# A two-block transformer in one program: four product tiles per norm, and the residual read from PSUM

## The chip, the cores and the metric

The kernel runs on one core of one Trainium2 chip. The metric is the device time in microseconds of the whole program. The runs of the kernel before took 2886.63 us in the median of three (2885.67 to 2890.1).

The core's engines run side by side and are joined by semaphores: TensorE (PE) multiplies, VectorE (DVE) and ScalarE (ACT) work elementwise and can read PSUM, GpSimd (POOL) works elementwise on SBUF, SyncE (SP) issues the DMAs. Each engine carries out its own program strictly in the order in which it is written.

## The reference, cut to what matters

Two blocks follow each other on 256 tokens of width 1024. The first has two layers, and carries 256 context tokens beside the 256 latent ones (512 columns in all, transposed: features on partitions, tokens on columns):

```python
for layer in range(2):
    x, ctx = ffn_sublayer(x, ...), ffn_sublayer(ctx, ...)        # f0, f2
    o = even_mixer(...) if layer == 0 else odd_mixer(...)        # DeltaNet and conformer / attention
    x = deepnorm_residual(x, mods[5] * o_lat, g, b)              # context too in layer 0
    x = ffn_sublayer(x, ...)                                     # f1, f3; context too in layer 0

def deepnorm_residual(x, y, g, b):
    return layer_norm(DEEPNORM_ALPHA * x + y, g, b)
def ffn_sublayer(x, shift, scale, gate, w_gu, w_down, g, b):
    y = swiglu(modulate(x, shift, scale), w_gu, w_down)          # 1024 -> 2 x 2816 -> 1024
    return deepnorm_residual(x, 0.5 * gate * y, g, b)
```

`modulate` is x * (1 + scale) + shift, `shift`, `scale` and `gate` come from a product of a condition vector with `ada_w`, 9 x 1024 values per layer. So behind each of the six sublayers stands: product, times gate, plus ALPHA times x (ALPHA is the square root of 2), layer norm over the features, modulation, next product. The second block has two layers with attention of three kinds, RMS norms and no ALPHA. All products are wanted in float32 quality.

## The kernel before, in words

**Products.** A weight tile is 128x128. Both the weights and the activations are split into a rounded high part and a rest, and `linear` issues three matmuls for each tile (lines 1570 to 1572: high by high, high by rest, rest by high). One output tile of 128 features takes 8 weight tiles (k = 0 to 7, or 22 in a down projection) and gathers in one of eight PSUM banks, handed out in turn by `Rot`.

**Weights.** All tiles come in the order of use from one stream in chunks of 1024 columns. A chunk has two halves of 512 columns, that is four tiles each. `take` hands out tiles; on entering a new half h it first yields a `load` (every second half) and then, through `splits_ahead`, the `split` of half h + 3, for there are four split buffers (NSPL) and the one it needs was used by half h - 1. A split is one ScalarE copy (line 1884) and one VectorE subtraction (line 2120; in the second block every second one is on GpSimd, line 2579).

**One order for all engines.** The generator `order` yields the steps of the whole program once, and each engine walks through the same list and carries out its part of every step. So the place of a step in `order` is its place in the program of every engine. What must not hold up the products is put into the list `later` and yielded by `run_later` behind the next `linear` or `pair`.

**Feed-forward `ffn` (f0 to f3).** First `pair` runs gate and up of tile m = 0 side by side: for each k a tile of the one, then of the other. Then for m = 1 to 21 `linear` gate, `linear` up, and `glu` (ScalarE Silu, line 1922, VectorE product, line 2202), and `dual`, the rounding of the result into its two parts (ScalarE line 1888, GpSimd line 2584). Then eight down projections of 22 k each. Beside the products a second generator, `ada_vec`, works out later modulation vectors on VectorE (line 2145); `linear` calls one piece of it at every fourth k (`pos["auto"]`), and ahead of m = 18 `drain` runs what is left. A sum on TensorE (line 1620) ends each group of 512 values.

**Residual.** Behind each down or output projection `residual`: ScalarE copies the bank times the gate column into a temporary (line 1916, two pieces of 256 columns where there are 512), VectorE forms ALPHA * x + t (line 2197), then `Sums.add` squares on ScalarE (line 1903) and adds up x and its square (GpSimd line 2588; for the last k VectorE, line 2156).

**Norm.** `Sums.finish`: column sums of both accumulators on TensorE into one bank with one signal (line 1630), `moments` on VectorE (mean line 2163, variance), square root on ScalarE (line 1911), reciprocal (line 2173), and two spreads, which bring a column back to all 128 partitions by TensorE (line 1636). Then for each k: VectorE subtracts the mean (line 2214), multiplies by the root's inverse (line 2220) and modulates 256 columns (line 2225), ScalarE the other 256 (line 1928), and `dual` rounds. `ln_update` turns X itself into the norm's output (line 1941) and goes into `later`; the eight of them stand behind the following `pair`.

**Even mixer.** After its norm `pair` runs the gate columns (`ab`) and `qkv_mm` 0; then for twelve tiles m: `short_conv` (ScalarE copies the bank, line 1960, VectorE five taps, lines 2304 and 2307, ScalarE Silu, line 1963), a part of the gate arithmetic on 64 partitions (`gate_chain`; a reciprocal at line 2252), the square and column sum of the tile before (`l2norm`), and one `linear` of `glu_v`, `glu_g` or `z`.

**Odd mixer.** `flush` runs the updates of X at once; then `load_memory` (SP, line 1537) loads the second block's memory into the half of X that the context held, and waits for the last update. `headnorm` runs `linear` for K0, then K1 (512 columns each), their squares and sums; V; later Q0 to Q7 with 256 columns.

## Time and profile before

| | |
|---|---|
| Median of three runs | 2886.63 us |
| Profiled execution | 2885.58 us, its span 2883.8 us |
| PE busy | 2680.6 us (93%) |
| DVE busy | 1731.7 us (60%) |
| ACT busy | 1260.8 us (44%) |
| POOL busy | 671.8 us (23%) |
| Products L1570 to L1572 | 3880 of each, 1344.2, 1313.4 and 1312.9 us |
| Splits, DVE L2120 | 838, 678.0 us |
| Splits, ACT L1884 | 1024 (of the ring), 623.6 us |
| Mean granted clock of TensorE | 0.949 |

PE's matmuls are pipelined, so the rows of successive ones overlap: in a full stretch one of 512 columns starts each 0.23 us though its row says 0.39. A row of the timeline is its start, its time, the engine, the line, the operation, output and inputs, and in brackets the idle time of the engine just before it with what released it. Rows of the same kind that follow each other are merged (xN).

### The profile page before, as it was taken

How to read it: one execution, taken by the hardware profiler on the slowest of the kernel's cores; microseconds unless marked ns; L12 is line 12 of the kernel's file. 1: busy time of each engine (PE TensorE's matmuls, PEld its weight loads, DVE VectorE, ACT ScalarE, POOL GpSimd, SP SyncE). 2: the span in 40 equal slices, each digit the busy share in tenths (PEclk: the TensorE clock that was granted, in tenths of full speed). 3: DMA queues.
4: the chain of work that ended last, by engine and by line, in shares of the span. 5: the costliest groups of instructions: out<-in, count | busy, mean ns of one | idle time of the engine just before them, and what ended most of it. 6: DMA issues, size and time to landing. Idle time of an engine off the chain costs nothing.

```text
span 2883.8 us, 43361 instructions
## 1 busy us (share of the span) xinstructions
PE 2680.6 (93%) x16824; PEld 2313.4 (80%) x16824; DVE 1731.7 (60%) x2978; ACT 1260.8 (44%) x2390; POOL 671.8 (23%) x608
## 2 busy tenths in 40 slices
PE   8999997988788999999999988989979999899998
PEld 5887886867776888887888867789978988898888
DVE  5775666778766765556554555565544656346666
ACT  3332326531255333334333345655545575454673
POOL 1111111012134111112111121021134424555224
PEclk9999998998788999998999988999979999899999
DMA  6553441210002543433443422245524434334334
GB/s 252 184 175 115 153 154 44 81 59 2 2 16 74 179 168 127 144 128 117 161 153 124 168 81 74 81 139 184 183 88 135 145 109 133 131 132 139 117 104 138
DMA packets 115868, 352.85 MB, mean 122 GB/s; under 512 B 12752, under 2 KB 14928, under 8 KB 115280
## 3 DMA queue, kind: packets, MB, share of 16 engines
q1 hardware_dynamic: 115664, 350.08, 36.1%
q8 instruction: 134, 2.20, 0.3%
q14 instruction: 70, 0.57, 0.1%
HBM read 348.98 MB, written 1.05 MB: 121 GB/s over the span
## 4 chain that ended last, share of the span: by engine, by line
PE 72%; DVE 12%; ACT 7%; issue 5%; POOL 3%; DMA 1%; SPq 0%; DVEq 0%; ACTq 0%; POOLq 0%
PE ps L1570 20%; PE ps L1572 19%; PE ps L1571 19%; ACT spl L1884 2%; PE ps L1620 2%; DVE spl L2120 1%; DVE big L2330 1%; PE ps L1636 1%; DVE work L2307 1%; PE ps L1838 1%; PE ps L1630 1%; DVE work L2225 1%; ACT big L2061 1%; POOL bigr L2584 1%; PE ps L1581 1%
## 5 line engine op out<-in xcount | busy, mean ns | idle before, releaser
L1570 PE MATMUL ps<-bigr,spl 128*128 128x256 f32 (+1 forms) x3880 | 1344.2, 346 | 69.9 <-issue 21.2
L1571 PE MATMUL ps<-bigr,spl 128*128 128x256 f32 (+1 forms) x3880 | 1313.4, 339 | 0.0
L1572 PE MATMUL ps<-bigr,spl 128*128 128x256 f32 (+1 forms) x3880 | 1312.9, 338 | 0.0
L2120 DVE TENSOR_TENSOR spl<-ring,spl 128x512 fp32r<-128x512 f32 x838 | 678.0, 819 | 652.8 <-ACT spl L1884 650.2
L1884 ACT ACTIVATE spl<-ring 128x512 fp32r<-128x512 f32 x1024 | 623.6, 625 | 763.8 <-PE ps L1572 606.2
L1570 PEld LDWEIGHTS ps<-bigr,spl 128*128 128x128 f32 x3880 | 750.4, 193 | 182.3 <-issue 44.7
L1571 PEld LDWEIGHTS ps<-bigr,spl 128*128 128x128 f32 x3880 | 752.4, 194 | 75.0 <-issue 2.2
L1572 PEld LDWEIGHTS ps<-bigr,spl 128*128 128x128 f32 x3880 | 750.9, 194 | 76.4
L2584 POOL TENSOR_TENSOR bigr<-work,bigr 128x512 fp32r<-128x512 f32 (+1 forms) x200 | 210.8, 1060 | 1026.5 <-ACT bigr L1888 1026.4
L2579 POOL TENSOR_TENSOR spl<-ring,spl 128x512 fp32r<-128x512 f32 x186 | 254.3, 1369 | 361.2 <-ACT spl L1884 360.9
L1888 ACT ACTIVATE bigr<-work 128x512 fp32r<-128x512 f32 (+2 forms) x232 | 120.5, 522 | 317.9 <-DVE work L2202 169.2
L2145 DVE SCALAR_TENSOR_TENSOR arow<-big,small,arow 128x512 f32<-128x512 f32 x196 | 150.1, 800 | 0.2
L2145 DVE SCALAR_TENSOR_TENSOR work<-big,small,work 128x512 f32<-128x512 f32 x196 | 145.1, 775 | 0.0
L2588 POOL TENSOR_TENSOR work<-work,X 128x512 f32<-128x512 f32 (+1 forms) x36 | 39.9, 1109 | 294.2 <-DVE X L2197 294.2
L2330 DVE SCALAR_TENSOR_TENSOR big<-big,prm 128x512 f32<-128x512 f32 x120 | 95.4, 828 | 0.0
L2202 DVE TENSOR_TENSOR work<-work,ps 128x512 f32<-128x512 f32 (+1 forms) x88 | 54.5, 619 | 52.0 <-PE ps L1572 33.1
L1838 PE MATMUL ps<-big 128*128 128x128 f32 (+2 forms) x288 | 60.4, 341 | 8.5 <-ACT big L2068 8.3
L1903 ACT ACTIVATE work<-X 128x256 f32<-128x256 f32 (+1 forms) x80 | 39.9, 502 | 64.4 <-DVE X L2197 35.0
L1630 PEld LDWEIGHTS ps<-cst,work 128*128 128x128 f32 x224 | 32.3, 218 | 43.6 <-issue 38.4
L1630 PE MATMUL ps<-cst,work 128*128 128x1 f32 x224 | 32.7, 266 | 36.8 <-DVE work L2156 15.5
L2588 POOL TENSOR_TENSOR work<-work 128x512 f32<-128x512 f32 (+1 forms) x48 | 59.4, 1238 | 14.4 <-ACT work L1903 14.4
L1819 PE MATMUL ps<-big 64*128 64x256 f32 (+2 forms) x192 | 61.7, 436 | 0.0
(291 smaller groups left out, 2506.6 us busy)
## 6 DMA issues: line engine op xcount, KB each, us to landing
ring<-w_stream SPq DMA_DIRECT2D x512, 512.0 KB, 3.4
big<-w_stream SPq DMA_DIRECT2D x256, 256.0 KB, 3.0
big<-w_stream SPq DMA_DIRECT2D x16, 512.0 KB, 11.0
X<-x_t SPq DMA_DIRECT2D x2, 1024.0 KB, 13.7
cst<-consts SPq DMA_DIRECT2D x1, 1601.5 KB, 7.3
X<-mem_t SPq DMA_DIRECT2D x1, 1024.0 KB, 5.7
out_t<-X SPq DMA_DIRECT2D x8, 128.0 KB, 2.1
prm<-params SPq DMA_DIRECT2D x1, 252.5 KB, 2.7
```

The costliest lines, as they stand in the source:

```text
L1570: pe.matmul(out, hi, x[0], start=k == 0, stop=False)
L1571: pe.matmul(out, hi, x[1], start=False, stop=False)
L1572: finish(pe.matmul(out, lo, x[0], start=False, stop=k == nk - 1), tile, key if k == nk - 1 else None)
L1630: ins = pe.matmul(b[:, at_ + t:at_ + t + 1], ap[:, 128 * t:128 * t + 128], P("ones")[:, 0:1], start=i == 0, stop=i == len(lst) - 1)
L1884: act.activation(hi_half(h), raw_half(h), ACTF.Copy).then_inc(*sig("hi", h))
L1888: act.activation(hi, raw, ACTF.Copy).then_inc(*sig("dhi", u))
L2120: dve.tensor_tensor(lo_half(h), raw_half(h), hi_half(h), SUB).then_inc(*sig("lo", h, by="lo_dve"))
L2145: ins = dve.scalar_tensor_tensor(acc[s], slot, c, acc[s], MUL, ADD)
L2330: ins = dve.scalar_tensor_tensor(two(CF[m]), YP[m][:, :, j:j + 256], a, two(CF[m]), MUL, ADD)
L2579: pool.tensor_tensor(lo_half(h), raw_half(h), hi_half(h), SUB).then_inc(*sig("lo", h, by="lo_pool"))
L2584: pool.tensor_tensor(lo, raw, hi, SUB).then_inc(*sig("dlo", u, by="dlo_pool"))
L2588: ins = pool.tensor_copy(dst, src) if copy else pool.tensor_tensor(dst, dst, src, ADD)
```

## The change

`pair` becomes `side_by_side`, which takes any number of outputs and their column counts. Behind a norm it now runs four tiles for each k: gate and up of m = 0 and 1 in `ffn`; `ab`, `qkv_mm` 0, `glu_v` 0 and `qkv_mm` 4 in the even mixer; in the odd mixer two, K0 (512 columns) and Q0 (256). The count over which `pos["auto"]` spreads the early work goes from 4 * (KF - 7) to 4 * (KF - 8).

`ln_update` writes ALPHA times the norm's output, with factors that `alpha_cols` forms in two VectorE operations; the first X is scaled by eight ScalarE copies (`first_scale`), deferred behind f0's first products. `residual` is now VectorE alone: x + gate * bank, 256 columns at a time, straight from PSUM.

The sums of x and of its square go into two banks with a signal each, the sum of x first, and the mean waits for its own alone. A dummy square root (`sqrt_table`) ahead of the down projections, of the odd mixer's output and of the second block's output loads the table early. In `short_conv` the Silu becomes a step of its own, `conv_silu`, yielded behind the next tile's copy.

```diff
-            def pair(key0, key1, w0, w1, src, n, between=None):
-                both = [banks.get() for _ in range(2)]
+            def side_by_side(keys, ws, src, n, between=None):
+                all_ = [banks.get() for _ in keys]
+                ns = n if isinstance(n, tuple) else (n,) * len(keys)
                 for k in range(len(src)):
...
-                    for (bank, free, bi), key, w in zip(both, (key0, key1), (w0, w1)):
+                    for (bank, free, bi), key, w, n in zip(all_, keys, ws, ns):
                         tile = yield from take(w(k))
...
-                    c = yield from columns(n, [(accQ, self.q)], [(accS, self.s)])
+                    bs, sfree, si = banks.get()
+                    us = new()
+                    yield "colsum", us, bs, [(accS, self.s)], n, sfree
+                    c = yield from columns(n, [(accQ, self.q)])
...
                 def update():
+                    yield "alpha_cols", u, ga, ba, g, b
                     for k in range(KD):
-                        yield "ln_update", u, k, n, g, b
+                        yield "ln_update", u, k, n, ga, ba
...
-                    pos["auto"] = 0, KD * len(early) + 2, 4 * (KF - 7)
+                    pos["auto"] = 0, KD * len(early) + 2, 4 * (KF - 8)
...
+                (k0, w0), (k1, w1) = gate_up(0), gate_up(1)
+                first = yield from side_by_side(k0 + k1, w0 + w1, src, n)
                 for m in range(KF):
...
-                    if m:
-                        bg, ig = yield from linear(("gate", f, m), wg, src, n)
-                        bu, iu = yield from linear(("up", f, m), wu, src, n)
+                    if m < 2:
+                        (bg, ig), (bu, iu) = first[2 * m:2 * m + 2]
...
                 if f == 0:
                     yield "tables",
+                yield "sqrt_table",
...
-                (bab, iab), first = yield from pair(
+                (bab, iab), first, first_v, second = yield from side_by_side(
+                    [("ab",), ("qkv_mm", 0), ("glu_v", 0), ("qkv_mm", 4)],
...
-                    yield "short_conv", m, cp, ci, b, free, ac, afree, (QK + V)[m], f0
+                    yield "short_conv", m, cp, ci, b, free, ac, afree
                     banks.give(bi, ("conv_in", m))
                     CP.give(ci, ("conv", m))
-                    tmps.give(ai, ("qkv", m))
+                    yield from conv_silu()
+                    silu.append((m, ac, ai))
                     yield from advance(chain_)
...
+                first, first_q = yield from side_by_side([("attn_in", 8), ("attn_in", 0)], [tile_of("attn_w_in", (0,), 128 * m) for m in (8, 0)],
+                                                         [(XM[k][0], XM[k][1], ms[k]) for k in range(KD)], (T, L))
                 for h in range(2):
-                    yield from headnorm(8 + h, T, "kn", K[h])
+                    yield from headnorm(8 + h, T, "kn", K[h], None if h else first)
...
-                dve.tensor_scalar(m, b[:, 4:4 + nb], 1.0 / count, None, MUL).then_inc(*sig("ln_mean", u))
+                dve.tensor_scalar(m, bs[:, 0:nb], 1.0 / count, None, MUL).then_inc(*sig("ln_mean", u))
...
-                w.wait_ge(*done("res_t", u))
                 w.all(xneed, done)
-                dve.scalar_tensor_tensor(x, x, ALPHA, t[:, 0:n], MUL, ADD).then_inc(*sig("res_x", u))
+                for s, a, b in halves(n):
+                    x = Xt[k][:, a:b]
+                    ins = dve.scalar_tensor_tensor(x, bank[:, a:b], gt[:, k, s:s + 1], x, MUL, ADD)
+                ins.then_inc(*sig("res_x", u))
```

## Rows read from the trace of the kernel before

**Rows 1.** The page's busy times.

```profile
PE 2680.6 (93%) x16824; PEld 2313.4 (80%) x16824; DVE 1731.7 (60%) x2978; ACT 1260.8 (44%) x2390; POOL 671.8 (23%) x608
```

**Rows 2.** Busy time by stretch: bounds, length, engines (x instructions), granted clock, DMA share, GB/s.

```profile
432.40:445.70 13.30, 7.07 (x33) 6.79 (x33) 8.26 (x21) 4.88 (x8) 1.26 (x1) 0.73 0.00 0
445.70:460.70 15.00, 10.93 (x36) 7.42 (x36) 13.31 (x20) 10.09 (x18) 9.72 (x9) 0.90 0.00 1
460.70:476.40 15.70, 11.17 (x48) 8.93 (x48) 8.00 (x14) 13.20 (x18) 2.37 (x5) 0.99 0.19 68
445.70:498.10 52.40, 42.05 (x165) 32.57 (x166) 35.19 (x51) 36.09 (x52) 12.08 (x13) 0.91 0.18 61
```

**Rows 3.** Timeline, f0's last residual and the norm's spreads.

```profile
432.48 0.84 ACT L1916 ACTIVATE work<-ps,small 128x256 f32<-128x256 f32 x2 [3.86 <-PE ps L1572]
433.35 0.69 DVE L2197 SCALAR_TENSOR_TENSOR X<-X,work 128x512 f32<-128x512 f32 x1 [4.00 <-ACT work L1916]
438.52 3.68 PE L1636 MATMUL ps<-cst,small 128*128 128x128 f32 x16 [0.26 <-DVE small L2163]
```

**Rows 4.** Timeline, the norm's steps for each k, then splits and updates.

```profile
451.35 0.95 DVE L2225 TENSOR_SCALAR work<-X,small 128x256 f32<-128x256 f32 x1
453.53 0.95 DVE L2225 TENSOR_SCALAR work<-X,small 128x256 f32<-128x256 f32 x1
...
458.51 2.17 ACT L1884 ACTIVATE spl<-ring 128x512 fp32r<-128x512 f32 x4
...
460.59 5.75 ACT L1941 ACTIVATE X<-X,prm 128x512 f32<-128x512 f32 x8
...
460.75 0.47 PE L1570 MATMUL ps<-bigr,spl 128*128 128x512 f32 x1 [2.53 <-DVE spl L2120]
```

**Rows 5.** VectorE by line and shape: a fused operation of 256 columns that reads PSUM.

```profile
L2449 DVE SCALAR_TENSOR_TENSOR work<-ps,prm,big 128x256 f32<-128x256 f32 x8 | 3.5, 479 | 1.7 <-PE ps L1810 1.7
```

**Rows 6.** Timeline, the odd mixer's last residual, and TensorE early in f3.

```profile
1886.93 0.41 DVE L2197 SCALAR_TENSOR_TENSOR X<-X,work 128x256 f32<-128x256 f32 x1
...
1912.17 0.39 PE L1570 MATMUL ps<-bigr,spl 128*128 128x256 f32 x1 [2.53 <-DVE spl L2120]
```

**Rows 7.** Timeline, the sums and the root in the second block's second layer.

```profile
2493.37 0.95 PE L1630 MATMUL ps<-cst,work 128*128 128x1 f32 x8
...
2493.97 1.28 ACT L1907 ACT_TABLE_LOAD   x1
...
2495.27 0.26 ACT L1907 ACTIVATE small<-ps,cst 128x2 f32<-128x2 f32 x1
```

**Rows 8.** Timeline, the first Silu of f2 and the rounding behind it.

```profile
1327.51 1.28 ACT L1922 ACT_TABLE_LOAD   x1
...
1330.16 0.63 ACT L1888 ACTIVATE bigr<-work 128x512 fp32r<-128x512 f32 x1 [0.75 <-DVE work L2202]
```

**Rows 9.** Timeline, the even mixer's first projections.

```profile
472.57 0.63 ACT L1963 ACTIVATE big<-work 128x512 f32<-128x512 f32 x1 [2.40 <-DVE work L2307]
...
476.44 0.80 PE L1570 MATMUL ps<-bigr,spl 128*128 128x512 f32 x1 [4.53 <-DVE spl L2120]
...
485.52 3.35 DVE L2252 RECIPROCAL big<-big 64x512 f32<-64x512 f32 x1
...
488.00 1.02 PE L1630 MATMUL ps<-cst,work 128*128 128x1 f32 x8 [1.71 <-ACT work L1903]
...
555.98 1.02 PE L1630 MATMUL ps<-cst,work 128*128 128x1 f32 x8 [0.82 <-ACT work L1903]
```

**Rows 10.** Timeline, the odd mixer: the memory's load, a split, the first column sum.

```profile
1715.89 0.66 SPq L1537 DMA_DIRECT2D X<-mem_t  x1
...
1722.90 0.63 ACT L1884 ACTIVATE spl<-ring 128x512 fp32r<-128x512 f32 x1 [6.56 <-DMA ring<-w_stream]
...
1724.15 1.02 PE L1630 MATMUL ps<-cst,work 128*128 128x1 f32 x8 [4.03 <-ACT work L1903]
```

**Rows 11.** Timeline, f0's drain of the early modulation work.

```profile
250.36 5.26 DVE L2145 SCALAR_TENSOR_TENSOR arow<-big,small,arow 128x512 f32<-128x512 f32 x6
...
255.67 3.57 PE L1620 MATMUL ps<-cst,arow 128*128 128x1 f32 x16 [6.02 <-DVE arow L2145]
```

More of the change, by code:

```diff
@@ L461, in spread, with columns @@
                 return b, ("spread", u), bi
-            def columns(n, squares, plain=()):
+            def columns(n, squares):
                 b, free, bi = banks.get()
@@ L827, in even_mixer @@
                 for n, m in enumerate((0, 4, 1, 5, 2, 6, 3, 7, 8, 9, 10, 11)):
-                    yield from qkv(m, first if n == 0 else None)
+                    yield from qkv(m, (first, second)[n] if n < 2 else None)
                     if normed:
@@ L840, in even_mixer @@
                         yield from cstep(3)
+                yield from conv_silu()
                 yield from flush()
@@ L1045, in even_mixer @@
                     if k == 0:
-                        both = yield from pair(("out", 0), ("out", 1), out_tile(0), out_tile(1), srcs, T, heads)
+                        both = yield from side_by_side([("out", 0), ("out", 1)], [out_tile(0), out_tile(1)], srcs, T, heads)
                         cols_.give(hi, ("hscale", 1))
@@ L1446, in order, with first_scale @@
                     ms.append([t])
-            xs = [[("x", k // 4)] for k in range(KD)]
+            xs = [[("x_scaled", k)] for k in range(KD)]
+            def first_scale():
+                for k in range(KD):
+                    yield "first_scale", k
+            later.append(first_scale)
             pos["unsplit"] = False
@@ L1911, in deviation, with sqrt_table, first_scale @@
                 act.activation(v, v, ACTF.Sqrt, bias=P(eps)).then_inc(*sig("sd", u))
-            def residual(u, k, n, t, bank, gt, need, xneed):
-                w.all(need, done)
-                for s, a, b in halves(n):
-                    ins = act.activation(t[:, a:b], bank[:, a:b], ACTF.Copy, scale=gt[:, k, s:s + 1])
-                ins.then_inc(*sig("res_t", u))
+            def sqrt_table():
+                act.activation(scratch, P("eps5"), ACTF.Sqrt)
+            def first_scale(k):
+                w.wait_ge(*done("first_mod", k))
+                act.activation(Xt[k], Xt[k], ACTF.Copy, scale=ALPHA).then_inc(*sig("x_scaled", k))
             def glu(f, m, t, bg, bu, free):
@@ L2080, in scalar_program @@
             run({f.__name__: f for f in (
-                tables, start, split, dual, evacuate, ada_row, square, root, deviation, residual, glu, ln_mod, ln_out, ln_update,
-                gates_in, gates_exp, gates_ratio, short_conv, conv_glu, z_silu, tail_columns, turn_kv, decay, unit_turn, q_decay,
+                tables, start, split, dual, evacuate, ada_row, square, root, deviation, sqrt_table, first_scale, glu, ln_mod, ln_out, ln_update,
+                gates_in, gates_exp, gates_ratio, short_conv, conv_silu, conv_glu, z_silu, tail_columns, turn_kv, decay, unit_turn, q_decay,
                 u_values, w_keys, tail_keys, scan_out, head_squares, conformer_silu, head_root, head_unit, scores, probs_turn, gated, index_head)})
```

87 lines of the change are left out of this document (51 added, 36 removed).

## Prediction, made before the change was run

> **What bounds the kernel now.** I read the page's busy times first: TensorE is busy 93% of the span [rows 1], so only the 203 us in which it isn't, and stretches at its lower clock, can be won or lost. The next view is the list of TensorE's own gaps in the timeline, with what each waited for. The change touches these places: the six layer norms (end of each feed-forward, f0 to f3, and of both mixers), the first projections behind five of them, the even mixer's projections, and the end of f0's early modulation work. In the norm behind f0 TensorE goes 13.3 us without a product [rows 2], because the last residual, the column sums, the two spreads and the first modulated tile are one chain [rows 3]. The products behind it then get 36 matmuls done in 15.0 us where 48 take 11.2 [rows 2]. The reader should see two different limits in those 15.0 us: VectorE delivers one k of X each 2.18 us [rows 4], and later the split weights run out: `take` splits a half only three halves ahead, all further splits stand in ScalarE's and VectorE's programs behind the whole norm, and TensorE waits 2.53 us for the first of them [rows 4]. The same 15.0 us come back in the norms behind the even mixer, f1 and f2.
>
> The profiled execution took 2885.58 us (span 2883.8 and 1.8 around it), the median of three is 2886.63; the sum is made against the former, and the 1 us between them is below anything argued here.
>
> **Part 1, residual from PSUM.** Removed: ScalarE's two copies, 0.84 us, and VectorE's 0.69 us [rows 3]. Added: two VectorE operations of 128x256 with a PSUM operand; the nearest row has 0.48 us for one [rows 5], and two that follow each other overlap a little, so 0.86 (bounds 0.80 and 0.96). On the chain into the norm that is 0.7 us less, behind f0, the even mixer, f1 and f2; behind f3 (256 columns, one copy instead of two) 0.45. Behind the odd mixer VectorE came from split weights and began the residual only at 1886.93 [rows 6], 0.7 us after ScalarE's copy, so I take nothing. The other 42 residuals lie beside products and gain nothing. Scaling X by the norm costs two tiny operations and a wait of ScalarE for them, counted in part 3; `first_scale` adds eight ScalarE copies at f0's start, about 5 us by the eight updates [rows 4], where ScalarE has three halves of slack: nothing, up to 2 us.
>
> **Part 2, column sums in two banks.** The mean can now be taken while TensorE sums the squares. The wait of the first spread for the mean, 0.26 us [rows 3], goes; the root isn't late, for the mean's spread takes half of 3.68 us [rows 3]. Six norms: 1.5 us. Parts 1 and 2 together: 4 x 0.95 + 0.70 + 0.25 = 4.75 us gained (bounds 3.5 and 7, the latter if the shorter gap keeps TensorE's clock up in the sums). The table load before the root is hidden everywhere but once, in the second block's second layer, where the root starts 1.3 us after the load [rows 7] and the sums had ended 0.95 us before it: 0.95 us gained. Here the row shows a load of 1.28 us and the root 0.02 us behind its end. The Trainium skill, ScalarE: Activation LUTs, section "What ACT_TABLE_LOAD costs", puts a drain of 1.38 us beside the load, 2.66 us for a switch; by that, an estimate from the page alone, this load's removal would bring 2.3 us instead of 0.95. The trace has no such drain between its rows, and the sum goes by the row.
>
> **Part 3, four tiles side by side.** In the norms with 512 columns, four tiles of 128 columns are exactly one half of weights for each k (before, two k shared a half). So the three halves at hand last for three k, not six: 36 matmuls in both cases. TensorE does them sooner, by k = 2, and then waits for the split that came at 460.75 [rows 4] and comes no earlier now. The three gaps of 0.5 us disappear and the 2.5 us one becomes 5.6: gain zero. That is the first step on which the forecast rests.
>
> The second: `side_by_side` now takes eight halves before its deferred work runs, so ScalarE has eight splits ahead of the norm's eight updates of X, and the last of these waits until TensorE has used the seventh half. In f1, counted from the restart at 460.75 of the same pattern: seventh half used 4 x 2.75 = 11.0 us later, split on both engines 1.4, factors 0.4, updates 5.75 [rows 4], table load, `silu`, product and rounding 3.3 (1327.51 to 1330.79) [rows 8], the same without load for the second tile 2.0, and only then the next split 1.3. Sum 25.1. TensorE has work for k = 3 to 7 and three more halves, 8 x 2.75 = 22.0 (21.8 by 0.2275 us for a matmul). It waits 3.3 us. Before there was no such wait, since only one tile's `silu` and four fewer splits stood ahead. Price 3.3 each in f1 and f2 (bounds 1 and 5), 6.6. In f3 the same happens with half the columns; there 2.53 us are lost today at that place [rows 6], so +0.8.
>
> In the even mixer what is queued ahead of the next split is longer: updates, gate sigmoid with its load, two convolution inputs, two exponentials waiting for VectorE, one `silu` waiting for a convolution, one square. From the same 460.75: factors ready at 473.5, updates to 479.3, sigmoid 481.2, first input 481.8, VectorE's convolution 485.4, its gate operations 486.9, exponential and second input 488.3, two loads, `silu` and exponential 491.6, square 492.2. The column sum of head 0 stands in TensorE's program behind eight tiles and waits for that square, from 479.9: 12.3 us idle. Behind it the next half waits until 497.1, because VectorE is in its 3.35 us reciprocal [rows 9]. At 498.1 TensorE has done 132 matmuls and one column sum; before it had 165 rows there [rows 2], which are 149 matmuls and eight each of one sum and one spread. So it is 17 x 0.23 + 1.05 = 4.9 us behind, although 4.53 + 1.71 us of today's waits there [rows 9] are part of that count. The deferred `conv_silu` takes ScalarE's wait of 2.40 us for each convolution away [rows 9]; from 498 on TensorE loses only 2.5 us to it in seven small gaps, the longest 0.82 [rows 9], nearly all won. Net +2.5 (bounds -6, if only a part of the queue is late, and +6).
>
> In the odd mixer two tiles (K0 and Q0) go side by side. Q0's 24 small matmuls fit under VectorE's 2.18 us per k. But the two tiles use up the four halves that K0 and K1 had, and the fifth half's data is stuck: its load stands in SP's program behind the load of the memory, which waits for the last update of X and goes out at 1715.89, and the weights arrive at 1722.9 [rows 10]. Before, K1 was done by 1720.1 and 4.03 us were lost until the column sum at 1724.15 [rows 10]. Now K1 starts at 1724.3 and takes 24 x 0.2275 and 1.2 for the lower clock: 1730.9, 6.8 later. Q0's 2.9 us are saved later, where TensorE waits for tiles of the memory anyway; I take 2.5. Net +4.3 (bounds 0.5 and 6.8).
>
> **Part 4, f0's early work.** `linear` calls one piece of it per four tiles, at most one, and `side_by_side` none. Before, 17 of the 18 column tiles ahead of the drain called it 68 times, and three vector steps were left, 5.26 us in a row [rows 11]; TensorE waited 6.02 us [rows 11]. Now 16 call it 64 times: six steps are left. Three more are 3 x 1.41 = 4.2 us; one sum (1.7 us, half of the 3.57 that it took at the lower clock [rows 11]) moves into that wait. Net +2.5 (bounds 2 and 5). f1 and f2 have fewer groups and end in time.
>
> **TensorE's clock.** Behind f0's norm the first gap brought the granted clock of the stretch to 0.73 of full speed, and even with 48 matmuls it was 0.99 in the next [rows 2]; the restart after 4.53 us shows 0.80 us for the first matmul, the one after 2.53 us 0.47 [rows 4, 9]. A restart at the lower of the two levels, 1.2 GHz, costs about six matmuls at 0.43 instead of 0.23, 1.2 us. The gap of 5.6 us behind three norms and the new waits in f1 and f2 can bring five such restarts: 0 to 6 us, I take 3. The Trainium skill, TensorE: Matmul & The Clock Gate, section "HAM oscillation — how this bites in real kernels", warns of this pattern, bursts of products with idle gaps between them where each burst starts cold; by it all five would fall and the time would be 3 us over my forecast. The rows say some do.
>
> **Sum.** -4.75 - 0.95 + 2.5 (f0) + 2.5 (even) + 6.6 (f1, f2) + 0.8 (f3) + 4.3 (odd) + 3 (clock) = +14. Forecast: 2900 us.
>
> **Rivals.** (a) Faster: the four tiles do fill the norm. This is one mechanism, split weights that reach further than three halves, or splits done in time between the norm's steps; it decides from the fourth k on. Then the gaps behind five norms (4.1 + 3.6 + 3.4 + 2.3 + 3, of which the first is in [rows 4]) and the even mixer's 8.7 go, with parts 1 and 2: about -25, or 2860 us. Against it: `take` decides the order, and 36 matmuls in the trace are exactly three halves. Chance 0.1. (b) The order is as I say, but the even and odd mixers gain: the deferred `silu` wins 6 us there instead of losing 2.5, and the memory's load costs nothing: -8.5 - 4 - 3 for the clock, 2884 to 2886 us, no change. For it: 4.53, 1.71 and 4.03 us of waits stand there today. Chance 0.2. (c) Half way between (a) and (b), where the shorter norm chain keeps the clock up in the sums and the new waits in f1 and f2 don't appear: about 2876 us. Chance 0.1. (d) All upper bounds: 2909 us. Chance 0.1. (e) My forecast: 0.5.
>
> **Numbers.** The range, from (b) with part of (c) to (d): 2876 to 2909. About 0.2% (5.8 us) is what a measurement can tell from no change: faster 0.2, same 0.17, slower 0.63.
>
> **What the profile would show.** Right: behind f1's norm one gap of about 5.6 us after 36 matmuls and another of 3 us after 132; a gap of 12 us before the first column sum of the even mixer; six vector steps in f0's drain; K1 of the odd mixer starting near 1724 plus the shift. Wrong: more than 36 matmuls before that gap, ScalarE splitting between the norm's steps, K1's weights landing before the memory's. If residual and sums save less than 0.7 us per norm, part 1 is mis-sized.

## The result: 30 us slower, twice what was forecast

The changed kernel takes 2916.58 us (2915.58 to 2917.13, four runs) against 2886.15 us (2884.45 to 2890.1): 1.0103 times the time before, 95% interval 1.0086 to 1.0121. The forecast was 2900, at most 2909. The profiled execution has a span of 2914.4 us and a mean granted clock of 0.942 (2883.8 and 0.949 before).

The page of the changed kernel, busy times, against [rows 1]:

```profile
PE 2689.9 (92%) x16824; PEld 2327.9 (80%) x16824; DVE 1730.3 (59%) x3020; ACT 1233.0 (42%) x2324; POOL 671.1 (23%) x608
```

TensorE has the same 16824 instructions and 9.3 us more in them; the rest of the 30.6 us is idle time. The same places set side by side, each measured in both traces between the starts of two waits of TensorE that both kernels have (us, after minus before; the first stretch begins at 0 and ends at the wait before f0's column sums):

| stretch | longer by | foreseen |
|---|---|---|
| f0, its drain among it | 3.4 | 2.5 |
| norm behind f0, even mixer to its last projection | 0.5 | 1.6 and a cold restart |
| rest of the even mixer | 2.1 | 0 |
| norm, f1 | 3.1 | 2.4 and a restart or two |
| norm, f2 | 6.6 | 2.4 and a restart or two |
| norm, odd mixer | 8.5 | 3.4 and a restart |
| norm, f3 | 3.2 | 0.6 |
| second block, layer 0 | 0.2 | -0.7 |
| second block, layer 1 | 3.0 | -0.95 |

The foreseen numbers sum to the forecast's 11 us without the clock's 3, the measured ones to the 30.6 us between the traces.

TensorE's new waits in the timeline of the changed kernel (start, length, engine, line, operation; in brackets the idle time before it and what ended that):

```profile
258.77 1.44 PE L1652 MATMUL ps<-cst,arow 128*128 128x1 f32 x6 [9.61 <-DVE arow L2180]
...
495.24 1.84 PE L1661 MATMUL ps<-cst,work 128*128 128x1 f32 x8 [12.09 <-ACT work L1934]
...
927.42 0.76 PE L1602 MATMUL ps<-bigr,spl 128*128 128x512 f32 x1 [4.56 <-DVE spl L2155]
...
954.50 0.79 PE L1602 MATMUL ps<-bigr,spl 128*128 128x512 f32 x1 [3.63 <-DVE spl L2155]
...
1331.16 0.77 PE L1602 MATMUL ps<-bigr,spl 128*128 128x512 f32 x1 [5.00 <-DVE spl L2155]
...
1359.39 0.50 PE L1602 MATMUL ps<-bigr,spl 128*128 128x512 f32 x1 [3.64 <-DVE spl L2155]
...
1732.83 0.77 PE L1602 MATMUL ps<-bigr,spl 128*128 128x512 f32 x1 [8.23 <-DVE spl L2155]
1740.09 0.77 PE L1602 MATMUL ps<-bigr,spl 128*128 128x512 f32 x1 [3.50 <-DVE spl L2155]
```

The waits are where the forecast put them: behind 36 products (4.56 and 5.00 us; 5.6 foreseen), behind 132 (3.63 and 3.64; 3.3), before the even mixer's first column sum (12.09; 12.3), and K1 starts at 1740.09, which is 1724.3 plus the 15.8 us by which everything was late by then. Behind f0's norm the first of these waits is 4.09 us. What the waits cost was not the sum of their lengths.

### The profile page after: what moved, and what is told of

Read it like the earlier page. It is cut to its first block, busy times and chain, and to the rows that moved or that the text cites. A ratio compares the mean times of both kernels' runs of the same rounds, so it can differ in the third digit from the quotient of the medians.

```text
span 2914.4 us, 43359 instructions
## 1 busy us (share of the span) xinstructions
PE 2689.9 (92%) x16824; PEld 2327.9 (80%) x16824; DVE 1730.3 (59%) x3020; ACT 1233.0 (42%) x2324; POOL 671.1 (23%) x608
## 4 chain that ended last, share of the span: by engine, by line
PE 72%; DVE 12%; ACT 7%; issue 5%; POOL 3%; DMA 1%; SPq 0%; DVEq 0%; ACTq 0%; POOLq 0%
PE ps L1602 20%; PE ps L1603 19%; PE ps L1604 19%; ACT spl L1915 2%; DVE spl L2155 2%; PE ps L1652 2%; PE ps L1667 1%; DVE big L2372 1%; PE ps L1661 1%; DVE work L2263 1%; PE ps L1869 1%; DVE X L2258 1%; ACT X L1974 1%; ACT big L2096 1%; POOL bigr L2626 1%
## 5 line engine op out<-in xcount | busy, mean ns | idle before, releaser
L2155 DVE TENSOR_TENSOR spl<-ring,spl 128x512 fp32r<-128x512 f32 x838 | 669.5, 807 | 692.1 <-ACT spl L1915 689.7
L1661 PE MATMUL ps<-cst,work 128*128 128x1 f32 x224 | 33.0, 267 | 43.5 <-DVE work L2191 12.7
```

The source lines that it names most:

```text
L1661: ins = pe.matmul(b[:, t:t + 1], ap[:, 128 * t:128 * t + 128], P("ones")[:, 0:1], start=i == 0, stop=i == len(squares) - 1)
L2155: dve.tensor_tensor(lo_half(h), raw_half(h), hi_half(h), SUB).then_inc(*sig("lo", h, by="lo_dve"))
```

## Which part costs what: four runs

**e1: residual, factor, sums and tables alone.** The four tiles are taken back everywhere:

```diff
-                (k0, w0), (k1, w1) = gate_up(0), gate_up(1)
-                first = yield from side_by_side(k0 + k1, w0 + w1, src, n)
+                k0, w0 = gate_up(0)
+                first = yield from side_by_side(k0, w0, src, n)
...
-                    pos["auto"] = 0, KD * len(early) + 2, 4 * (KF - 8)
+                    pos["auto"] = 0, KD * len(early) + 2, 4 * (KF - 7)
```

> The changed kernel with its feed-forwards and the even mixer back to two tiles behind the norm, the odd mixer back to one, and each silu of the even mixer directly behind its convolution: the residual from PSUM, the factor in X, the column sums in two banks and the early root tables are what is left of the change. My sum gives -4.75 - 0.95 against before: 2880.5 us, and the clearest sign is 0.95 us less in each norm's chain and the 6.02 us drain of f0 as before. Rival (the norms gain as much, but restarts of TensorE at its lower clock, which depend on where each gap falls, take it back somewhere else): 2884 to 2888 us, with the gaps still shorter. If parts 1 and 2 carry a part of the 30 us that the whole change lost, over 2890.

Measured: 2888.66 us against 2884.8 (ratio 1.0021, 1.0007 to 1.0035), 3.9 slower by the medians; the ten runs lie between 2881.95 and 2896.88 us, and the interval of the ratio is 2 to 10 us. The gain in the norm's chain is there: f1 and f2 with their norms are 1.3 and 1.8 us shorter than before. It is given back in places that I had costed at nothing or at a gain. Timeline of e1, ScalarE behind the norm of f0 and late in the second layer:

```profile
462.47 0.81 ACT L1972 ACTIVATE X<-X,small 128x512 f32<-128x512 f32 x1 [2.45 <-DVE small L2265]
...
478.33 0.79 PE L1600 MATMUL ps<-bigr,spl 128*128 128x512 f32 x1 [5.62 <-DVE spl L2153]
...
2848.83 1.28 ACT L1943 ACT_TABLE_LOAD   x1
2850.12 0.20 ACT L1943 ACTIVATE small<-cst 128x1 f32<-128x1 f32 x1
2850.23 1.14 ACT L1913 ACTIVATE spl<-ring 128x512 fp32r<-128x512 f32 x2
...
2852.26 0.39 PE L1600 MATMUL ps<-bigr,spl 128*128 128x256 f32 x1 [0.55 <-POOL spl L2619]
```

The factors (L2265) stand in VectorE's program behind the low halves of the splits, so ScalarE's updates wait 2.45 us for them, where before they followed the splits at once, and TensorE's 4.53 us of [rows 9] become 5.62. The early root table is loaded between two splits of a stretch in which TensorE lives from split to split: a new wait of 0.55 us. The layer's last 96 us are 2.3 us longer, but only 1.4 of them lie behind the load (from the product at 2849.66 to the last sums 25.42 us, before 24.04). The other 0.9 lie ahead of it, behind a wait of 2.56 us that both kernels have: the granted clock of the next 10 us is 0.50 and 0.90 here, 0.67 and 1.00 before. In the same layer the early table does bring the 0.9 us that I had foreseen at the norm (a wait of 1.46 becomes 0.55), and the next wait for a split grows from 1.51 to 3.13.

f0 is 0.9 us longer, with two new waits, 0.74 and 1.47 us, that end at 66.85 and 71.34 us. The rows lead back to `first_scale`: its eight copies (4.26 us from 47.71) stand ahead of the first Silu, so VectorE waits 3.16 us for that one at 52.63 and comes late to the early modulation step at 55.82. A load of SP's queue waits for this step (7.8 us, before 5.1), the next weights are loaded behind it, and the split waits 9.54 us for them where it waited 7.00. No run moved these copies. The waits stay in the other kernels with two tiles in f0 and these copies, e3, e4, e5 (0.74 and 1.48) and e8, and are neither in the kernel before nor in those with four tiles in f0. From the product that stands at 38 us on, f0 is 2.5 us longer than before; that its sum shows only 0.9 is chance, for TensorE is at that product 1.6 us earlier, and this start differs by up to 2.2 us between these kernels.

**e2, e3, e4: one site each** of tiles side by side on top of e1: all feed-forwards; the even mixer with its later `silu`; K0 with Q0.

> As e1_parts12, but with the four tiles side by side in all four feed-forwards (and the modulation steps that go with them); both mixers stay as before. The trace of the changed kernel has 3.6 us more in f0's drain and 3.1, 6.7 and 3.2 us more in f1, f2 and f3, parts 1 and 2 deducted already. If the places add up, this kernel is 16.6 us above before and about 19 to 22 above e1_parts12: 2901 to 2903 us. Rival (f2's 6.7 were a chance of the clock behind the shifts of the mixers): 2896 or less. My prediction had 9.9 plus part of the clock for this part alone: 2892 us.

Measured: 2908.22 us against the same 2884.8 (ratio 1.0078, 1.0062 to 1.0094), 19.6 more than e1, as the theory had it. By places it is 2.4 us more than e1 in f0, 4.4, 8.4 and 2.7 in f1, f2 and f3. f1 and f2 are 3.1 and 6.6 us longer than before, as in the whole change: f2's 6.6 isn't a matter of what the mixers do.

> As e1_parts12, but with the four tiles side by side and the later silu in the even mixer alone. The change's trace shows this mixer 0.5 us longer with parts 1 and 2 in it, so its own price is about 1.5 us: e1_parts12 + 1.5. My sum had +2.5 and one cold restart more. Rival: the later silu and fewer small gaps win more than the 12 us wait costs once the following stages are not shifted: e1_parts12 - 2. The 12 us wait before the first column sum has to be there in either case.

Measured: 2890.06 us (ratio 1.0020, 1.0010 to 1.0029), 1.4 more than e1, which the spread of the runs can't tell from nothing; in the traces the mixer with its norm is 2.4 us longer than in e1. The wait of 12.09 us is there (1.84 us of column sums at 494.01 behind it), and the mixer has no other that is new.

> As e1_parts12, but with K0 and Q0 side by side in the odd mixer alone. The change's trace has the norm and the odd mixer 8.5 us longer with 0.7 us gained by parts 1 and 2 in it. By its rows there are two waits instead of the one that I counted: the fourth half's split stands behind all eight updates of X (8.2 us of wait), then K1's data stands behind the memory's load (3.5 us). If that is the whole cause: e1_parts12 + 9. My sum: + 4.3. Rival (the order of the queues costs little, and the loss came from the lower clock behind f2): + 3 or less.

Measured: 2893.46 us (ratio 1.0030, 1.0020 to 1.0040), 4.8 more than e1. The odd mixer is 5.0 us longer than in e1, with waits of 8.22 and 3.12 us. Nearer to my 4.3 than to the 9. There is a third wait that I had not counted, 5.00 us before a column sum at 1769.49 (5.01 at 1787.77 in the whole change); with its neighbours it makes 8.2 us where e1 has 6.0 in five pieces. In the whole change the stretch is 8.5 us longer than before. Of the 3.6 us between that and e4, 3.3 stand behind this same wait: to the next wait of 2.3 us it is 61.3 us there and 58.0 in e4, at a granted clock of 0.64 and 0.89 in the first 12 and the next 20 us against 0.78 and 1.00. Why the clock differs behind the same wait is open.

Parts and whole agree: 3.9 + 19.6 + 1.4 + 4.8 = 29.7 us, measured 30.4. That it is so close is in part luck, for e1, which stands in every difference, is known to a few us only.

## Why the waits cost more than their length

**e10: the clock behind the waits.** Useless products (no result is read) in the four waits of f1 and f2:

```diff
+                    if k == 2 and keys[0] in (("gate", 1, 0), ("gate", 2, 0)):
+                        yield from warm(16)
...
+                    if k == 3 and key in (("up", 1, 2), ("up", 2, 2)):
+                        yield from warm(12)
```

> The changed kernel, with products of no use put into TensorE's waits in f1 and f2: 16 of 128x512 behind the 36th product of the norm's tiles (a gap of 4.6 and 5.0 us in the trace) and 12 behind the fourth k of the tile in which the second gap stands (3.64 us). They end before the awaited weights come, so they change nothing but the clock. If the lower clock behind these gaps is the part of f1 and f2 that the gaps don't explain (14 us at 0.84 and 15 us at 0.91 in f2, 14 us at 0.93 in f1), it comes back: 3 to 4.5 us less than the changed kernel. Rival (the clock there doesn't depend on the gaps, or useless products cost as much as they win): within 1 us of it, or slower.

Measured: 2907.68 us against 2885.45 (ratio 1.0076, 1.0059 to 1.0092), 22.2 above before where the change is 30.4: 8.2 less, about twice what the theory had. f1 and f2 fall from 3.1 and 6.6 us above before to 0.3 and 0.7, together 8.8 us. Busy time by stretch (bounds, length, TensorE busy and rows, weight loads, VectorE, ScalarE, GpSimd, granted clock, DMA share and GB/s): the changed kernel behind the wait of 4.56 us, and in the column sums behind f1; then the same two places in e10.

```profile
927.42:931.00 3.58, 3.58 (x10) 2.87 (x11) 1.66 (x3) 0.00 (x0) 0.00 (x0) 0.58 0.66 181
931.00:950.87 19.87, 19.86 (x88) 16.09 (x86) 3.61 (x7) 10.99 (x16) 0.11 (x1) 1.00 0.29 100
...
1305.64:1309.00 3.36, 3.36 (x17) 3.36 (x18) 1.52 (x8) 0.00 (x0) 0.00 (x0) 0.53 0.00 0
```

```profile
930.78:934.36 3.58, 3.58 (x16) 2.99 (x17) 1.66 (x3) 0.57 (x1) 0.00 (x0) 1.00 0.70 192
...
1306.15:1308.10 1.95, 1.95 (x17) 1.95 (x18) 1.44 (x8) 0.00 (x0) 0.00 (x0) 1.00 0.00 0
```

In the changed kernel TensorE works as soon as the wait is over, but at 1.2 GHz: in 3.58 us it has 10 rows, in e10 16. Then it is at 2.4 GHz for the rest. In the rows of the timeline the products behind the four waits start 0.43 us apart instead of 0.23, six to eight of them behind three waits and twelve behind the one of 5.00 us. That costs 1.5, 1.6, 2.6 and 1.7 us, 7.3 in all. In e10, where 0.9 to 1.0 us is left of each wait, it is 0.1 us each. The difference, 6.9 us, is what f1 and f2 are shorter by in e10 from the norm's first product on. The other 1.9 of the 8.8 us lie ahead of both waits of f2, in column sums and spreads that ran at the lower clock in the changed kernel (3.34 us of sums, in e10 1.92); no useless product stands near them, so e10 doesn't show what brought this. So a wait of 3.6 to 5 us costs 1.5 to 2.6 us on top of itself. That agrees with the pattern in the Trainium skill, TensorE: Matmul & The Clock Gate, section "HAM oscillation — how this bites in real kernels": the burst behind a gap starts cold.

The kernel before paid this too: its waits of 2.54 and 2.53 us at 923.75 and 1321.91 are followed by six to eight such products, 1.4 and 1.6 us, while the one of 2.53 us at 460.75 [rows 4] is followed by none. Of the 7.3 us the change brought 4.3.

**e6: what the second wait is made of.** Four tiles everywhere; updates of X one by one, and the factors before the down products:

```diff
-                def update():
-                    yield "alpha_cols", u, ga, ba, g, b
-                    for k in range(KD):
-                        yield "ln_update", u, k, n, ga, ba
+                def update(k=0):
+                    yield "ln_update", u, k, n, ga, ba
+                    if k < KD - 1:
+                        later.append(lambda: update(k + 1))
```

> The changed kernel with its four tiles everywhere, but the factors early and ScalarE's eight updates of X one by one behind the following products (behind f2 all of them still stand ahead of the odd mixer), not in a row in front of the next split. Theory: the second wait in f1 and f2 (3.64 us each) and its cold restart are the updates' work, the first (4.56 and 5.00 us) is the order of the splits behind the norm. Then the second wait and 5 us of the even mixer's 12.1 us go and the first shrinks by the 0.4 us of the factors at most: 2 x 4.5 + 3 + 5 = 17 us less than the changed kernel, about 2900. Rival (the silus and duals alone fill ScalarE long enough): the second wait stays above 1.5 us and the total is above 2908.

Measured: 2890.64 us against 2885.11 (ratio 1.0023, 1.0011 to 1.0034), 5.5 above before where the change is 30.4: 25 less. Behind f1 the wait of 5.00 us stays (5.01) and the one of 3.64 is gone; before the even mixer's column sum 12.09 become 6.12. The updates were the second wait; the first is the order of splits and norm.

**e5: parts 1 and 2 repaired.** e1 with the factors before the down products and without the second block's early root table:

```diff
+                yield from factors(*ln, xs[KD - 1])
                 for k in range(KD):
                     b, bi = yield from linear(("down", f, k)
...
-                    yield "sqrt_table",
                     for k in range(KD):
                         b, bi = yield from linear(("w_out", l, k)
```

> As e1_parts12, with two repairs: VectorE makes the norm's 16 factor columns before the down product's loop (in the trace of e1_parts12 ScalarE waits 2.45 us for them behind the low halves of the splits in front of the updates of the even mixer, 1.28 us in f3), and the second block has no early root table (there a load of 1.28 us at 2848.83 stands between splits, and the layer's last 96 us take 2.3 us longer). If these two are why parts 1 and 2 gained nothing: 1.9 + 1.3 + 1.4 to 2.3 less than e1_parts12 (2888.7), some 2883. Rival (a new phase of the clock is all there is, 2 us more or less anywhere): 2887 to 2890, with the second layer still over 2 us longer than before.

Measured: 2882.52 us against 2885.11 (ratio 0.9993, 0.9984 to 1.0003): 6 less than e1, with the second layer as long as before to 0.2 us and the even mixer with the norm ahead of it 3.2 us shorter. So these two placements cost most of what parts 1 and 2 lost. Against e1 the three places that they touch are 3.7, 2.0 (f3) and 2.8 us (second layer) shorter, 8.5 in all, more than the 6 of the medians; the trace of e5 gives back 3.7 us in the odd mixer, 2.1 of them in its norm's column sums and spreads at the lower clock. With the two repairs parts 1 and 2 gain 2.6 us, which this measurement can't tell from nothing.

**e13: the drain.** The whole change with one edit in f0, so that no modulation step is left over:

```diff
-                        if (i + 1) * steps // of > i * steps // of:
-                            yield from pump()
+                        yield from pump((i + 1) * steps // of - i * steps // of)
...
-                    pos["auto"] = 0, KD * len(early) + 2, 4 * (KF - 8)
+                    pos["auto"] = (0, 9 * len(early) + 2, 4 * (KF - 6)) if f == 0 else (0, KD * len(early) + 2, 4 * (KF - 8))
```

> The changed kernel with one edit: f0's early modulation work gets 74 steps in the 64 calls ahead of the drain, where one per call left nine over (six of them vector steps). My prediction priced the longer drain at 2.5 us, the trace shows 3.6 (9.61 against 6.02 us). If the drain is pure loss, all 9.6 us go: 2907 us. Rival (VectorE has the same work and TensorE waits for it, or for splits behind it, inside f0): half of it or less, 2911 to 2916.

Measured: 2901.41 us against 2884.07 (ratio 1.0054, 1.0039 to 1.0069), 17.3 above before where the change is 30.4: 13.1 less, more than the wait of 9.61 us: f0 is 12.7 us shorter than in the change. The timeline of the changed kernel has five of the six vector steps in a row in the drain, two operations each (the first step stands just before), and its stretches show the clock behind it:

```profile
250.42 8.29 DVE L2180 SCALAR_TENSOR_TENSOR arow<-big,small,arow 128x512 f32<-128x512 f32 x10
```

```profile
249.50:260.00 10.50, 1.23 (x6) 1.23 (x6) 8.77 (x13) 0.68 (x2) 1.70 (x1) 0.58 0.54 173
260.00:300.00 40.00, 40.00 (x166) 33.26 (x166) 11.85 (x17) 10.62 (x18) 3.13 (x3) 0.90 0.24 79
```

In the 40 us behind the drain the changed kernel has 12 rows less than e13, at 0.23 us each some 3 us. The same stretches of e13:

```profile
249.50:260.00 10.50, 10.50 (x56) 8.96 (x55) 3.51 (x5) 2.42 (x4) 1.29 (x1) 1.00 0.28 101
260.00:300.00 40.00, 40.00 (x178) 33.12 (x177) 14.21 (x19) 14.80 (x25) 5.15 (x4) 1.00 0.29 100
```

## Can four tiles fill the norm? My rival (a), built

**e7 and e8: norm steps and splits interleaved.** With four tiles (e7) and with two (e8). `layer_norm` no longer issues its eight steps in a row; `side_by_side` asks for step k+1 before it takes the weights of k, and `take` puts the next split behind it. Updates and factors as in e6, no early table in the second block, K0 alone in the odd mixer. `pos["pool"]` does one thing more: while the norm's steps are interleaved, every second split has its low half on GpSimd (three behind f1's norm, 1.3 us each), which takes that work off VectorE. No run has the new order without it:

```diff
-                first = yield from side_by_side(k0 + k1, w0 + w1, src, n)
+                first = yield from side_by_side(k0 + k1, w0 + w1, src, n, norm_between)
...
+            def norm_between(k):
+                pos["pool"] = True and bool(ahead)
+                yield from norm_to(k + 1)
```

> Four tiles in the feed-forwards and the even mixer, one in the odd mixer, with the norm's steps and the splits interleaved in the queues (step k+1, then the split three halves ahead), the updates of X one by one behind later products, all modulation steps of f0 done before the drain, factors early, no early root table in the second block. If the order of the queues is why four tiles don't fill the norm, TensorE works through from the first modulated tile: the gaps of 4.6 to 5.0 and 3.6 us behind f1, f2 and the even mixer's norm are gone, the drain of 9.6 is under 3, and the time is that of my rival (a), 2860 (2855 to 2868). If VectorE's 2.2 us per k plus the low half of a split can't follow 12 products of 2.7 us, small gaps of 0.3 to 0.5 us per k are left: 2868 to 2875.

Measured: 2867.03 us against 2885.11 (ratio 0.9941, 0.9924 to 0.9959). f1, f2 and f3 are 3.3, 5.3 and 5.1 us shorter than before, the even mixer with its norm 10.3 up to its last projection (and 3.2 longer behind it); f0 is 5.3 us longer, since 74 modulation steps in 52 calls are too dense: TensorE waits 1.76, 2.25 and 2.01 us for sums there.

> As e7_lazy4, but with two tiles side by side as in the kernel before (and each silu of the even mixer directly behind its convolution). It tells the worth of the four tiles once the order is right. Two tiles give TensorE 1.37 us of work per k against VectorE's 2.18 to 2.87: 0.8 to 1.5 us idle for each of eight k behind three norms, 20 to 36 us more than e7_lazy4, of which the later products get nothing back. Theory: 2880 or more. Rival (tiles don't matter, only the waits for splits did): within 3 us of e7_lazy4.

Measured: 2877.56 us (ratio 0.9974, 0.9963 to 0.9985), 10.5 more than e7, a third to a half of what the arithmetic of the idle time per k gave. With the right order the four tiles are worth 10 us; in the order of the change they cost 21 (19.6 and 1.4), of which 2.4 are f0's drain.

**e9, e11, e12: three more edits,** each on the one before. e9 puts f0's modulation steps evenly, also behind each k of `side_by_side`; e11 issues the memory's load behind K1's weights; e12 adds K0 and Q0 side by side, interleaved:

```diff
-                yield "load_memory", xs[KD - 1]
...
                 for h in range(2):
                     yield from headnorm(8 + h, T, "kn", K[h])
+                yield "load_memory", xs[KD - 1]
```

> As e7_lazy4, but f0's early modulation steps are spread evenly: one behind each of the first eight k of the four tiles, then one per four weight tiles, 74 steps in 72 calls, so that none is left for the drain. e7_lazy4 ran 74 steps in its first 52 calls, and its trace shows waits of 1.76, 2.25, 0.49, 0.72 and 2.01 us in the first 230 us and the norm behind f0 5.3 us later than before, though the drain itself had gone. If VectorE's pace is what matters, these waits go too and f0 ends 5 us earlier than before: some 10 us less than e7_lazy4, 2857 us. Rival (each group's sum has to wait for VectorE at any pace): half of it, 2862.

Measured: 2870.3 us against 2885.45 (ratio 0.9948, 0.9933 to 0.9963), 3 more than e7: a miss. f0 is 6.4 us shorter than in e7, but f1 and f2 are 3.3 and 4.7 longer: they have modulation steps of their own, and these now stood between the steps of the norm.

> As e9_pumps, with the load of the odd mixer's memory issued behind the weights of K1 instead of ahead of the first tile. The one edit is the place of a transfer in SP's queue. In the trace of before TensorE waits 4.03 us there and ScalarE's split waits 6.56 us for data. If the load's place is the cause: 3 to 4 us less than e9_pumps, with the memory in time for its own sums. Rival (the column sum of K0 is late for another reason, or the memory comes late now): no change, or a new wait of 2 us or more where the memory is first squared.

Measured: 2864.19 us (ratio 0.9928, 0.9913 to 0.9943), 6.1 less than e9, all of it in the odd mixer with its norm (1.8 above before, then 5.1 below). That is more than the 3 to 4 us foreseen. The wait of 4.03 us of [rows 10], 4.09 in e9, is gone: the load's place was its cause.

> As e11_memory_late, with K0 and Q0 side by side and interleaved with the norm's steps and the splits, the updates of X directly behind them. In e4_odd2 the same two tiles in the change's order cost 4.8 us. If that was the order of the queues (the fourth half's split behind the updates, K1's data behind the memory), it turns into a gain of Q0's 24 small products, about 2 to 3 us less than e11_memory_late. Rival (what follows Q0 waits for the memory anyway): no change.

Measured: 2867.44 us (ratio 0.9939, 0.9925 to 0.9954), 3.3 more than e11: the mixer loses 5.5 us. Even in the better order the two tiles side by side don't pay there. Whether the later updates or the memory's later load does it wasn't tried.

**e14 and e15.** e14 is e11 with e13's modulation steps in f0 and none behind the norm's tiles. e15 adds 6 and 13 useless products of 128x128 in the two waits of each norm.

> e11_memory_late without the modulation steps behind the norm's tiles, which e9_pumps had brought into f1 and f2 as well: its trace has f1 and f2 3.3 and 4.7 us longer than e7_lazy4, since VectorE had those steps between the norm's. 74 steps in 64 calls in f0, as in e13_pumps_after; f1 and f2 as in the changed kernel. If the steps in the norm were the cause, f1 and f2 come back to e7_lazy4's length: 8 us less than e11_memory_late in all, f0 2 us either way: 2856 (2854 to 2860). Rival (f1 and f2 were longer through the clock alone): 2862 to 2865.

Measured: 2842.48 us against 2884.07 (ratio 0.9849, 0.9834 to 0.9864), the fastest of all: 1.5% below the kernel before. f1 and f2 are 5.7 and 5.8 us shorter than before (0.0 and 0.6 in e11), f0 9.1. It is 20 us less than e11 where I expected 8, a miss on the good side: f1 and f2 came back by 10.9 us, and f0, for which I had allowed 2, is 7.3 us shorter, so the modulation steps behind the first tiles' k cost in f0 as well. The odd mixer is 2.6 us shorter, which no run explains.

> As e14_best, with products of no use in the two waits of each norm that are left: 6 of 128x128 in the 1.79 us before the column sums, 13 in the 3.52 us before the first modulated tile. e10_warm gave 8.9 us for four gaps, so the lower clock behind a gap is a cost of its own. The granted clock in the 10 us behind a norm is 0.79 to 0.86 in the changed kernel: if that comes from the norm's waits, each of six norms gives back 1 to 2 us: 6 to 10 us less than e14_best. Rival (the column sums and spreads between keep the clock low in any case, or the useless products run at the lower clock and end late): within 1 us of e14_best, or slower.

Measured: 2842.77 us (ratio 0.9851, 0.9834 to 0.9868): no difference from e14. The useless products do what they should to the clock. Stretches from the first product behind the even mixer's norm, e14 and then e15:

```profile
890.55:900.60 10.05, 10.05 (x35) 8.12 (x36) 6.35 (x11) 5.24 (x9) 4.73 (x4) 0.78 0.15 53
900.60:905.60 5.00, 5.00 (x22) 3.82 (x22) 3.74 (x5) 1.47 (x4) 2.92 (x3) 1.00 0.33 105
```

```profile
885.96:896.01 10.05, 9.33 (x41) 7.35 (x40) 7.19 (x10) 5.54 (x10) 6.86 (x6) 1.00 0.16 53
896.01:901.01 5.00, 3.92 (x18) 2.89 (x16) 4.93 (x7) 2.25 (x4) 1.82 (x2) 1.00 0.31 105
```

At 0.78 TensorE is busy for all 15 us and has 57 rows; at 1.00 it has 59 and waits 1.8 us, and each of these waits ends with GpSimd's low half of the next k of X: the chain through VectorE, ScalarE and GpSimd delivers X no faster. Here the slow clock is hidden by the norm's own pace; behind the waits of e10, where all of X is there, it isn't.

## The prediction, step by step

- **The order of the work** (three halves ahead, splits behind the norm, updates ahead of the splits, K1 behind the memory): right. Each wait stands where it was put, to about 1 us in length (1.5 behind f0's norm). I missed one more in the odd mixer: the fourth half's split also stands behind the eight updates, 8.23 us, before K1's 3.50; K1's start, and with it the price (4.8 measured, 4.3 in the sum), hardly changes.
- **f1 and f2, 3.3 each:** the second wait was 3.6. With the clock held up (e10) the two lie 0.3 and 0.7 above before, 1.6 and 2.5 above e1's: less than my 3.3 each. With the clock as it was they lie 4.4 and 8.4 above e1's (e2): what was too small is the clock's share. The first wait, at 4.6 to 5.0, was shorter than my 5.6.
- **f3, 0.8:** mis-sized, 2.7 between e1 and e2. The waits are 2.95 and 5.11 us where 1.86 and 2.53 stood [rows 6]; of the second, 1.4 us are the late factors, for e1 has 3.91 there. I had taken half of f1's price less what is lost there today. In e6, with the updates spread, they are 3.71 and 0.66: here too the updates are the later one.
- **Even mixer, +2.5:** right in mechanism, and in size as far as it can be told (1.4 by the medians, 2.4 in the traces).
- **f0's drain, +2.5:** somewhat too small. Its wait is 3.6 us longer; f0 as a whole is 2.7 (e2) to 3.8 us (the change) longer than before from 39 us on. The whole drain costs 13 us, not 9.6.
- **The clock, 3:** too small. I priced a restart at six products at half speed, 1.2 us; behind the four waits of f1 and f2 it is 1.5 to 2.6, and against before that is 4.3 us more. The 3.3 us in the odd mixer come on top: 7.6, over my upper bound of 6. The column sums of the norms don't enter: from the last residual's wait to the first product it is 10.4 us ahead of f1 and 12.3 ahead of f2 now, and 12.8 and 12.2 before. And I took fewer restarts than there were gaps over 3 us, though the section of the Trainium skill that I cited beside it (TensorE: Matmul & The Clock Gate, "HAM oscillation — how this bites in real kernels") has each burst start cold.
- **Parts 1 and 2, -5.7:** the largest error, and of the wrong sign, +3.9. The chain did get shorter, but I gave placements no cost: the factors, "counted in part 3", stand behind the splits (a wait of ScalarE of 2.45 us in the even mixer, 1.28 in f3); the table load, counted as a gain of 0.95, brings 0.9 at the norm and costs 1.6 at the next wait for a split and 1.4 where it stands between splits; and `first_scale`, "nothing, up to 2 us", brings waits of 2.2 us in f0 as long as two tiles run there.

By the medians of e1 to e4, parts 1 and 2 missed by 9.6 us and the feed-forwards by 9.7 (6.7 with the clock's 3 put there), the even mixer by -1.1 and the odd one by 0.5: 9.6 + 6.7 - 1.1 + 0.5 = 15.7 of the 16.4 us between the 14 of my sum and the 30.4 measured. So two steps failed: that parts 1 and 2 bring a gain wherever they are placed, and the price of TensorE's clock behind the new waits. The likeliest case had the right mechanism for the waits themselves.

The range has an error of its own. Case (d) is called "all upper bounds" and put at 2909 us, but the bounds that the parts state add up to more: -3.5 - 0.95 + 5 + 6 + 10 + 0.8 + 6.8 + 6 = 30, which is 2916 us, and 2918 with the 2 us of `first_scale`. The measured 2916.58 lies there, by luck, for parts 1 and 2 are far outside their bounds and the even and the odd mixer well inside. Rival (a) is off as well: its items and parts 1 and 2 make 31, so 2855 us and not 2860.

Open: why the same code in the second block, behind the same wait of 2.56 us, gets a granted clock of 0.50 and 0.90 in the next two stretches of 5 us in e1 and the change, and 0.67 and 1.00 in the kernel before. It is the 0.9 us ahead of the table load; e2, e3 and e4 have it too (0.7 to 0.8), e5, without the early table, has not. Whether the early table at the layer's start brings it, by shifting what follows, was not tried.

## What to carry to other kernels

Where one engine's program carries the steps that release the next stage and the steps that refill it, count every instruction ahead of the refill, tiny ones and table loads too: an edit "beside other work" is free only if nothing that it delays is on a queue to the bound engine. Wider work behind a chain only helps if its operands are prepared between the links of that chain (e6 won 25 us by order alone; of e7's further 24, some 13 lie at the norms, where a few splits on GpSimd helped too). And price a wait of TensorE of 3 us or more at its length plus what the restart takes: 1.5 to 2.6 us here.

## What the runs showed of the hardware

Behind a wait of TensorE of 3.6 to 5.0 us the next six to twelve products of 512 columns start 0.43 us apart instead of 0.23, which costs 1.5 to 2.6 us. The length of the wait alone doesn't decide it: of three waits of 2.53 and 2.54 us in the kernel before, two are followed by such products and one by none. Useless products in the wait win the time back if no other engine sets the pace (6.9 us for four waits in e10, nothing in e15). An ACT_TABLE_LOAD takes 1.28 us in the rows and the next ScalarE operation starts at its end (2848.83 to 2850.12); no further drain shows.
